# Folding the dt projection straight into token order, with the softplus on 128x16

## The chip, the cores and the metric

The program runs on one core of one Trainium2 chip. The metric is the device time of one execution in microseconds; the figure for a kernel is the median of its runs.

## The reference

One sequence of 256 tokens, 1,024 wide, goes through two transformer blocks in float32. The first block has two mixers side by side (an SSD mixer and an RWKV7 mixer) on one input projection, then an output projection and a gated feed-forward of 2,816. The second has HGRN2 and block attention, cross attention over a memory of 256 tokens, and a feed-forward of 4,096. The change touches one thin piece of the SSD mixer, the step size dt of its 8 heads:

```python
xn = _rms_norm(h, pre_mix_norm[l]); proj = xn @ w_in[l]
z, xbc, dt = jnp.split(p, [SSD_D, SSD_D + SSD_CONV_DIM], axis=-1)   # dt: 256 tokens x 8 heads
dt = jax.nn.softplus(dt + dt_bias)
A = -jnp.exp(a_log)
X = xh * dt[..., None]            # the mixer's values, scaled per token and head
a = dt * A                        # its cumulative sum over a chunk of 128 tokens gives all decays
```

## The kernel before

Everything is a hand-placed program: each engine runs a fixed list of instructions, and they wait for one another on semaphores (`mark` counts a step, `at` gives the value that it reached, `wait_ge` waits). The order of the work is the order of the calls at the end of the listing for each engine (from L3362 for ScalarE, from L3459 for VectorE), and nothing is reordered at run time. Activations lie with features on the partitions and 256 tokens along the free dimension, in tiles of 128 features. A weight is loaded in float32 in chunks of up to 2 MB into a ring of four slots, by one queue (SyncE's, L482 to L497); ScalarE makes the high float16 half (L539), VectorE the low half (L571), and TensorE multiplies each tile in three float16 products (L625). A chunk's slot is given back when its last reader is done, and only then is the next chunk's load issued.

The input projection runs tile by tile in the order k, lora, r, v, xs, bc, z (L814, `pe_project1`). The results leave PSUM by `evacuate1` on VectorE (L1036), a bank of two tiles at a time, and ScalarE (`act_kept`, L1076) and VectorE (`dve_shift`, L1083) do the token shift of the RWKV part. Between the tiles TensorE does small steps of the mixers whose inputs are ready: the dt fold (L913) after the third r tile, the low-rank products (L1637), the norms of the keys (`pe_head_norm`, L1661), the turning of v (L1790).

The dt part goes in these steps:
- After the lora tiles, 8 float32 products (L966), one for each 128 rows of the weight, go to four groups of 32 partitions of bank 5; products 0 to 3 to the left half, 4 to 7 to the right half. The 8 heads are the last 8 of each 32 columns.
- VectorE scales both halves by the norm into `dt_parts`, 128x512 (L1049).
- `pe_dt_fold` (L913) adds the four groups and the two halves by two products with a piece of the identity as weights and 256 columns moving; dt then has 8 heads on partitions and 256 tokens along.
- ScalarE adds the bias (L1134), between `act_kept(act, 2)` and the split of the xs weights (L3383). Later `act_dt`, `act_dt_log` and `dve_dt` make the softplus and the product with the rate on tiles of 8x256: four operations on ScalarE (L1140, L1141, L1143, L1148), of which one is on the 8 rates, and five on VectorE (L1166 to L1179).
- `pe_ssd` turns dt and its product with the rate into token order by four transposes (L1200, L1201), after the first z tile, and `dve_ssd` copies them out (L1268) before it scales the values (L1273). TensorE sums over tokens at L1215, after the second z tile; VectorE copies the sums out (L1279), and the decays follow from them (L1190, L1288, L1360, L1364, L1294), while the z tiles fill TensorE (L901).

`parameter_table` packs all small parameters, then x and the memory in feature order, then the final gain, in one tensor with 128 rows of 21,888 bytes. The small parameters are its first 352 columns; x begins at byte 1,408 of a row. x is loaded in three pieces at the start (L455), the memory's features by L496.

Of the kernel before, what the change touches and what calls it, by code (L numbers as in the profile page):

```python
# [17 lines left out]
ALU = mybir.AluOpType  # L18
# [5 lines left out]
P = 128  # L24
T = 256
# [37 lines left out]
    ("ssd_conv_w", 4 * 8), ("ssd_conv_b", 8), ("ssd_norm", 4), ("ssd_d", 4),  # L63
    ("ssd_dt_bias", 1), ("ssd_a_log", 1),
    ("rwkv_mu", 14), ("rwkv_w0", 4), ("rwkv_a0", 4), ("rwkv_k_k", 4), ("rwkv_k_a", 4),
# [9 lines left out]
PARAM_COLS = _n  # L75
X_AT, MEM_AT, FINAL_AT = PARAM_COLS, PARAM_COLS + KT * T, PARAM_COLS + 2 * KT * T

# [65 lines left out]
def parameter_table(inputs):  # L143

    def tiles(a):
        return np.asarray(a).reshape(-1, P).T

    def column(a):
        out = np.zeros((P, 1), np.float32)
        out[:a.shape[0], 0] = a  # L150
        return out

    a = {k: np.asarray(v) for k, v in inputs.items()}
    mu = a["rwkv_mu"][0]
    cols = {name: None for name, _ in PARAM_TILES}
    for name in cols:
        if name == "rwkv_mu":
            k0 = RW_D + 64
            al = 3 * RW_D + 64
            order = [mu[k0:k0 + RW_D], mu[RW_D:k0], mu[al:al + 64], mu[al + 64:], mu[:RW_D],  # L160
                     mu[k0 + RW_D:k0 + 2 * RW_D]]
            cols[name] = tiles(np.concatenate(order))
        elif name == "ssd_conv_w":
            cols[name] = np.concatenate([tiles(a[name][0, i]) for i in range(4)], axis=1)
        elif name == "ffn_conv_w":
            cols[name] = np.concatenate([tiles(a[name][0, i]) for i in range(3)], axis=1)
        elif name == "lb_logits_2":
            cols[name] = np.concatenate([tiles(a[name][i]) for i in range(2)], axis=1)
        elif name == "ssd_d":
            cols[name] = tiles(np.repeat(a[name][0], SSD_D // SSD_HEADS))  # L170
        elif name in ("ssd_dt_bias", "ssd_a_log"):
            cols[name] = column(a[name][0])
        else:
            cols[name] = tiles(a[name].reshape(-1))
        assert cols[name].shape[1] == dict(PARAM_TILES)[name], name
    def turned(rows):

        return rows.T.reshape(KT, P, T).transpose(1, 0, 2).reshape(P, KT * T)

    return np.ascontiguousarray(np.concatenate([*cols.values(), turned(a["x"][0]), turned(a["mem_2"][0]),  # L180
                                                np.broadcast_to(a["norm_final_2"].reshape(1, D), (P, D))], axis=1))
# [129 lines left out]
def build(nc, w, out, known):  # L311

    with ExitStack() as ctx:
# [15 lines left out]
        def halves(b):  # L329
            return banks[b][:, :].rearrange("p (i t) -> p i t", i=2)  # L330
# [21 lines left out]
        def const(name):  # L352
            a, n = CONST_AT[name]
            return consts[:, a:a + n]
# [61 lines left out]
        BTOKS = view(SOLVE + 5152, 2, SSD_STATE)  # L416
        dtT, aT, dtmp = view(SOLVE + 7168, T), view(SOLVE + 5664, T), view(SOLVE + 5920, T)
        dt_parts = view(SOLVE + 5664, 2, T)
        dtok = view(SOLVE + 6176, NC_, 8)
        atok = view(SOLVE + 6192, NC_, 8)  # L420
        cstok = view(SOLVE + 6208, NC_, 8)
        dect = view(SOLVE + 6224, 8)
        acol = view(SOLVE + 6232, 2)
        GT = A_[:, 0:2, :].rearrange("p a (b t) -> p (a b) t", t=C)
# [483 lines left out]
        def pe_dt_fold(pe):  # L908

            pe.wait_ge(*at("dt raw"))  # L910
            pe.wait_ge(*at("constants landed"))
            for i in range(2):
                mm = nc.tensor.matmul(banks[6][0:SSD_HEADS, 0:T], const("ident32")[:, BASE - SSD_HEADS:BASE],  # L913
                                      dt_parts[:, i, :], start=(i == 0), stop=(i == 1))
            mm.then_inc(*mark("proj1_dt", "dt folded"))

        def pe_project1(pe):
            pe_project1_first(pe)
            for i, (kind, j) in enumerate(TILE_OF):
# [42 lines left out]
                if kind == "lora" and j == 1:  # L962

                    for k in range(KT):
                        q = BASE * (k % 4)
                        mm = nc.tensor.matmul(halves(5)[q:q + BASE, k // 4, :], slot("w_in", "lora")[:, k, 232:264],  # L966
                                              hg[:, k, :], start=True, stop=True, tile_position=(0, q))
                    mm.then_inc(*mark("proj1_dt", "proj1 dt"))
# [70 lines left out]
        def dve_project1_rwkv(dve):  # L1039
            lora_low(dve)  # L1040
            dve.wait_ge(*at("pre_mix", "rstd"))
            for b in range(7):
# [4 lines left out]
                if b == 2:  # L1047
                    dve.wait_ge(*at("proj1 dt"))
                    nc.vector.scalar_tensor_tensor(dt_parts, halves(5), 1.0 / W_SCALE, over(rstd[:, :], 2), ALU.mult,  # L1049
                                                   ALU.mult).then_inc(*mark("dt_raw", "dt raw"))  # L1050
                if b in (0, 2):
                    split_low(dve, b // 2, range(4))
                if b == 3:
                    split_low(dve, 2, range(4))
                if b == 4:
                    dve_shift(dve, range(3))
                    bc_low(dve, (0, 1))
# [71 lines left out]

        def act_dt_bias(act):  # L1130

            act.wait_ge(*at("parameters landed"))
            act.wait_ge(*at("dt folded"))
            nc.scalar.activation(dtT[0:8, :], banks[6][0:SSD_HEADS, 0:T], ACT.Identity,  # L1134
                                 bias=par("ssd_dt_bias", 0)[0:8, :]).then_inc(*mark("dt_act", "dt biased"))

        def act_dt(act):

            act.wait_ge(*at("dt biased"))
            nc.scalar.activation(dtmp[0:8, :], dtT[0:8, :], ACT.Abs).then_inc(*mark("dt_act"))  # L1140
            nc.scalar.activation(acol[0:8, 0:1], par("ssd_a_log", 0)[0:8, :], ACT.Exp).then_inc(*mark("dt_act"))  # L1141
            act.wait_ge(*so_far("dt_act"))
            nc.scalar.activation(dtmp[0:8, :], dtmp[0:8, :], ACT.Exp, scale=-1.0).then_inc(*mark("dt_act", "dt exp"))  # L1143

        def act_dt_log(act):
            act.wait_ge(*at("dt one plus"))
            act.wait_ge(*at("mem", "squares", 1))
            nc.scalar.activation(dt_log, aT[0:8, :], ACT.Ln).then_inc(*mark("dt_act", "dt log"))  # L1148

# [11 lines left out]

        dt_log = sqs[0:8, 0, 0:T]

        def dve_dt(dve):
            dve.wait_ge(*at("dt exp"))
            nc.vector.tensor_scalar(aT[0:8, :], dtmp[0:8, :], 1.0, None, ALU.add).then_inc(  # L1166
                *mark("dt_vector", "dt one plus"))
            dve.wait_ge(*so_far("dt_vector"))

            nc.vector.scalar_tensor_tensor(dtmp[0:8, :], aT[0:8, :], -1.0, dtmp[0:8, :], ALU.add,  # L1170
                                           ALU.subtract).then_inc(*mark("dt_vector"))
            dve.wait_ge(*so_far("dt_vector"))
            nc.vector.scalar_tensor_tensor(dtT[0:8, :], dtT[0:8, :], 0.0, dtmp[0:8, :], ALU.max,
                                           ALU.subtract).then_inc(*mark("dt_vector"))
            dve.wait_ge(*so_far("dt_vector"))
            dve.wait_ge(*at("dt log"))
            nc.vector.tensor_tensor(dtT[0:8, :], dtT[0:8, :], dt_log, ALU.add).then_inc(*mark("dt_vector"))
            dve.wait_ge(*so_far("dt_vector"))
            nc.vector.tensor_scalar(aT[0:8, :], dtT[0:8, :], acol[0:8, 0:1], -1.0, ALU.mult, ALU.mult).then_inc(  # L1179
                *mark("dt_vector", "dt done"))  # L1180
# [13 lines left out]
        def pe_ssd(pe):  # L1194

            pe_z_tile(pe, 0)
            pe.wait_ge(*at("dt done"))
            pe.wait_ge(*at("v token-major", 1))
            for c in range(NC_):
                nc.tensor.transpose(banks[4][:, 8 * c:8 * c + 8], dtT[0:8, c * C:(c + 1) * C], ident[0:8, 0:8])  # L1200
                mm = nc.tensor.transpose(banks[4][:, 16 + 8 * c:24 + 8 * c], aT[0:8, c * C:(c + 1) * C],  # L1201
                                         ident[0:8, 0:8])
            mm.then_inc(*mark("ssd_pe", "ssd dt turned"))

            pe.wait_ge(*at("kk unit"))
# [6 lines left out]
            pe_z_tile(pe, 1)  # L1212
            pe.wait_ge(*at("ssd dt token-major"))
            for c in range(NC_):
# [51 lines left out]
        def dve_ssd(dve):  # L1266
            dve.wait_ge(*at("ssd dt turned"))
            nc.vector.tensor_copy(view(SOLVE + 6176, 32), banks[4][:, 0:32]).then_inc(  # L1268
                *mark("ssd_vector", "ssd dt token-major"))
            dve.wait_ge(*so_far("ssd_vector"))  # L1270
            for c in range(NC_):
# [2091 lines left out]
        def _(act):  # L3363
# [18 lines left out]
            act_kept(act, 2)  # L3382
            act_dt_bias(act)  # L3383
            split_high(act, 2, range(4))
# [171 lines left out]
```

## Time and profile before

| | us |
|---|---|
| median of 3 runs | 738.62 |
| lowest and highest run | 738.46, 740.3 |
| the profiled execution, its own time | 738.89 |
| span of the profiled execution (first to last instruction) | 737.1 |

| engine | busy us | share of the span |
|---|---|---|
| DVE (VectorE) | 563.7 | 76% |
| ACT (ScalarE) | 435.1 | 59% |
| PEld (TensorE weight loads) | 593.8 | 81% |

The granted clock of TensorE is 1.00 over the whole span. All places are given in us from the start of the span. PE is TensorE's matmuls, POOL is GpSimd, SP is SyncE, which only issues transfers. Matmuls are pipelined: the length shown for one is longer than the distance to the next, so for TensorE the distances between starts are read. L12 is line 12 of the kernel; where a helper is used by several steps, its line stands for all of them.

### The profile page before, as it was taken

What the parts mean: (1) busy time and instruction counts of PE and PEld (TensorE: products, weight loads), DVE (VectorE), ACT (ScalarE), POOL (GpSimd) and SP (SyncE); (2) the same over time, 40 slices, a digit from 0 to 9 for tenths busy, and PEclk for the clock granted to TensorE, in tenths of its full rate; (3) what the DMA queues carried; (4) which work ended last, traced back from release to release, by engine and by line L of the source; (5) the groups of instructions that cost most, each with busy time, mean ns of one, the idle gap of its engine ahead of it and who ended that gap; (6) DMA issues with size and microseconds to landing.
All of it is one profiled execution on the core that took longest, in us unless ns stands there. A gap on an engine that the chain in (4) does not pass through costs nothing.

```text
span 737.1 us, 16447 instructions
## 1 busy us (share of the span) xinstructions
PE 727.0 (99%) x7048; PEld 593.8 (81%) x7048; DVE 563.7 (76%) x895; ACT 435.1 (59%) x689; POOL 49.4 (7%) x83
## 2 busy tenths in 40 slices
PE   9999999999999999999999999999999999999997
PEld 6888878889778888888877695898888888865553
DVE  5699977777889999997568797889685676762453
ACT  5599863524748667666556572487483755653342
POOL 0000143040020000000002000003003000000000
PEclk9999999999999999999999999999999999999999
DMA  9990305321666655665780742338336264566001
GB/s 317 397 406 9 114 18 192 155 67 53 217 240 228 205 181 189 227 217 184 269 303 26 289 146 113 116 121 337 116 112 232 99 213 171 207 229 232 25 1 58
DMA packets 67145, 129.50 MB, mean 176 GB/s; under 512 B 3968, under 2 KB 28032, under 8 KB 66816
## 3 DMA queue, kind: packets, MB, share of 16 engines
q1 hardware_dynamic: 66032, 126.07, 47.4%
q0 software_dynamic: 320, 1.67, 0.7%
q8 instruction: 56, 0.92, 0.5%
q10 hardware_dynamic: 720, 0.70, 0.3%
q14 instruction: 17, 0.14, 0.1%
HBM read 127.39 MB, written 1.05 MB: 174 GB/s over the span
## 4 chain that ended last, share of the span: by engine, by line
PE 82%; DVE 9%; ACT 4%; DMA 3%; SPq 2%; issue 1%; ACTq 0%; DVEq 0%
PE bank L625 38%; PE bank L747 14%; PE bank L3200 11%; PE bank L2526 3%; PE bank L1569 3%; DMA ring<-in_w_in_dram 3%; PE bank L1550 2%; DVE arena L571 2%; PE bank L1828 1%; SPq L496 1%; PE bank L901 1%; DVE arena L1083 1%; PE bank L2006 1%; ACT arena L539 1%; DVE arena L613 1%
## 5 line engine op out<-in xcount | busy, mean ns | idle before, releaser
L625 PE MATMUL bank<-hg,arena 128*128 128x256 f16 x2496 | 275.0, 273 | 0.2 <-DVE hg L650 0.2
L625 PEld LDWEIGHTS bank<-hg,arena 128*128 128x128 f16 x2496 | 243.9, 98 | 30.5 <-issue 1.1
L571 DVE SCALAR_TENSOR_TENSOR arena<-ring,arena 128x1024 f16<-128x1024 f32 x150 | 175.6, 1226 | 60.2 <-ACT arena L539 60.2
L539 ACT ACTIVATE arena<-ring 128x1024 f16<-128x1024 f32 x150 | 146.7, 1044 | 87.9 <-PE bank L3200 37.6
L3200 PE MATMUL bank<-arena 128*128 128x512 f16 (+1 forms) x480 | 83.6, 336 | 0.0
L3200 PEld LDWEIGHTS bank<-arena 128*128 128x128 f16 x480 | 47.0, 98 | 36.1
L747 PE MATMUL bank<-arena 128*128 128x256 f16 x528 | 57.8, 273 | 0.0
L747 PEld LDWEIGHTS bank<-arena 128*128 128x128 f16 x528 | 51.7, 98 | 6.0
L558 DVE SCALAR_TENSOR_TENSOR arena<-ring,arena 128x2048 f16<-128x2048 f32 x22 | 50.4, 2292 | 0.7
L747 PE MATMUL bank<-mix,arena 128*128 128x256 f16 x384 | 42.2, 273 | 0.0
L551 ACT ACTIVATE arena<-ring 128x2048 f16<-128x2048 f32 x22 | 41.7, 1894 | 0.0
L747 PEld LDWEIGHTS bank<-mix,arena 128*128 128x128 f16 x384 | 37.6, 98 | 4.3
L625 PE MATMUL bank<-xv,arena 128*128 128x256 f16 x336 | 37.4, 273 | 0.0
L2434 DVE SCALAR_TENSOR_TENSOR arena<-arena,params 128x256 f32<-128x256 f32 x88 | 36.7, 479 | 0.7 <-ACT arena L2477 0.7
L625 PEld LDWEIGHTS bank<-xv,arena 128*128 128x128 f16 x336 | 32.6, 98 | 4.9 <-issue 0.7
L2477 ACT ACTIVATE arena<-arena,params 128x256 f32<-128x256 f32 x44 | 20.0, 500 | 27.7 <-DVE arena L2423 27.7
L3154 DVE SCALAR_TENSOR_TENSOR arena<-bank,rstd 128x512 f32<-128x512 f32 x16 | 11.0, 690 | 24.0 <-PE bank L625 16.9
L640 ACT ACTIVATE hg<-h,params 128x256 f16<-128x256 f32 x32 | 15.9, 498 | 22.2 <-DVE h L2963 11.8
L660 POOL TENSOR_TENSOR ssum<-sqs 128x256 f32<-128x256 f32 x4 | 2.9, 728 | 350.0 <-ACT sqs L644 350.0
L650 DVE SCALAR_TENSOR_TENSOR hg<-h,params,hg 128x256 f16<-128x256 f32 x32 | 20.4, 658 | 4.4 <-ACT hg L640 4.4
L1569 PE MATMUL bank<-arena,xk 128*128 128x512 f16 x96 | 21.4, 379 | 0.0
L2526 PE MATMUL bank<-arena,hg 128*128 128x512 f16 x96 | 21.2, 379 | 0.0
(419 smaller groups left out, 974.0 us busy)
## 6 DMA issues: line engine op xcount, KB each, us to landing
ring<-in_w_in_dram SPq DMA_DIRECT2D x12, 2048.0 KB, 9.3
ring<-in_ffn_w_up_dram SPq DMA_DIRECT2D x22, 1024.0 KB, 7.3
ring<-in_w_ff_dram SPq DMA_DIRECT2D x8, 2048.0 KB, 9.1
ring<-in_w_ff_dram SPq DMA_DIRECT2D x16, 1024.0 KB, 6.6
ring<-in_ffn_w_down_dram SPq DMA_DIRECT2D x11, 1024.0 KB, 5.5
ring<-in_w_out_dram SPq DMA_DIRECT2D x8, 1024.0 KB, 7.8
ring<-in_w_xk_dram SPq DMA_DIRECT2D x2, 2048.0 KB, 11.2
ring<-in_w_xv_dram SPq DMA_DIRECT2D x2, 2048.0 KB, 10.7
```

The source lines that it names most:

```text
L539: nc.scalar.activation(quarter(halves_of(chunk)[0], chunk, q), quarter(slot(*chunk), chunk, q), ACT.Copy, scale=W_SCALE).then_inc(*mark("w ...
L551: nc.scalar.activation(pair_of(halves_of(chunk)[0], chunk, q), pair_of(slot(*chunk), chunk, q), ACT.Copy, scale=W_SCALE).then_inc(*mark("w ...
L558: nc.vector.scalar_tensor_tensor(pair_of(halves_of(chunk)[1], chunk, q), pair_of(slot(*chunk), chunk, q), W_SCALE, pair_of(halves_of(chunk ...
L571: nc.vector.scalar_tensor_tensor(quarter(halves_of(chunk)[1], chunk, q), quarter(slot(*chunk), chunk, q), W_SCALE, quarter(halves_of(chunk ...
L625: mm = nc.tensor.matmul(out_, weight[a][:, k, cols], src[:, k, b, :], start=(first and i == 0), stop=(last and i == 2), skip_group_check=True)
L650: nc.vector.scalar_tensor_tensor(hg16[:, m, 1, :], h[:, m, :], par(gain, m), hg16[:, m, 0, :], ALU.mult, ALU.subtract).then_inc(*mark("nor ...
L747: mm = nc.tensor.matmul(out_, weight, moving[:, k, b, :], start=(first and n == 0), stop=(last and n == 2), skip_group_check=True)
L1569: mm = nc.tensor.matmul(banks[2 + c][:, :], mem16[:, k, x, c * C:(c + 1) * C], w_[a][:, k, :], start=(k == 0 and i == 0), stop=(k == KT - ...
L2434: nc.vector.scalar_tensor_tensor(uacc[r][:, i, :], uraw[r][:, i, tap:tap + T], par("ffn_conv_w", 2 * FFT * tap + tile0 + i), uacc[r][:, i, :],
L2477: nc.scalar.activation(uacc[r][:, i, :], uraw[r][:, i, 2:T + 2], ACT.Copy, scale=par("ffn_conv_w", 2 * 2 * FFT + 2 * p + FFT * (b % 2) + i ...
L2526: mm = nc.tensor.matmul(banks[bank][:, :], hg16[:, k, b, c * C:(c + 1) * C], w_[a][:, k, :], start=(k == 0 and n == 0), stop=(k == KT - 1 ...
L3200: mm = nc.tensor.matmul(last_bank(c, half, cols)[:, cols], hid2[:, k, x, c * C:(c + 1) * C], weight[a][:, k % 4, 512 * half + cols.start:5 ...
```

## The change

- The products 4 to 7 of dt are added in PSUM to the products 0 to 3 (same four groups of partitions, one half of the bank). `dt_parts` is 128x256 instead of 128x512.
- The fold takes `dt_parts` as weights, 128 tokens at a time, and 8 columns of the identity piece as the moving side. So dt comes out with 128 tokens on the partitions, and 2 chunks x 8 heads along: 128x16.
- The bias is added by VectorE (`dve_dt_bias`), after the evacuation of bank 4 of the projection and before its token shifts; the ScalarE step is gone.
- The softplus and the product with the rate run on 128x16; the rate's exponential on 128x8.
- The four transposes, the copy out and their waits are gone; "dt done" is waited for after the second z tile, and by VectorE before it scales the values. ScalarE's logarithm no longer waits for the memory's squares, whose buffer it used.
- The bias and the rate stand in 8 columns each, repeated on all 128 partitions. The small parameters are now 366 columns, x begins at column 384 (byte 1,536), and a row has 22,016 bytes. 14 more columns are loaded with the small parameters (L3366).

```diff
-    ("ssd_dt_bias", 1), ("ssd_a_log", 1),
+    ("ssd_dt_bias", SSD_HEADS), ("ssd_a_log", SSD_HEADS),
...
-X_AT, MEM_AT, FINAL_AT = PARAM_COLS, PARAM_COLS + KT * T, PARAM_COLS + 2 * KT * T
+X_AT = (PARAM_COLS + 63) // 64 * 64
+MEM_AT, FINAL_AT = X_AT + KT * T, X_AT + 2 * KT * T
...
-            for i in range(2):
-                mm = nc.tensor.matmul(banks[6][0:SSD_HEADS, 0:T], const("ident32")[:, BASE - SSD_HEADS:BASE],
-                                      dt_parts[:, i, :], start=(i == 0), stop=(i == 1))
+            for c in range(NC_):
+                mm = nc.tensor.matmul(banks[6][:, 8 * c:8 * c + 8], dt_parts[:, c * C:(c + 1) * C],
+                                      const("ident32")[:, BASE - SSD_HEADS:BASE], start=True, stop=True)
...
-                        mm = nc.tensor.matmul(halves(5)[q:q + BASE, k // 4, :], slot("w_in", "lora")[:, k, 232:264],
-                                              hg[:, k, :], start=True, stop=True, tile_position=(0, q))
+                        mm = nc.tensor.matmul(banks[5][q:q + BASE, 0:T], slot("w_in", "lora")[:, k, 232:264],
+                                              hg[:, k, :], start=(k < 4), stop=(k >= 4), tile_position=(0, q),
+                                              skip_group_check=True)
...
                 if b == 4:
+                    dve_dt_bias(dve)
                     dve_shift(dve, range(3))
...
-        def act_dt_bias(act):
-
-            act.wait_ge(*at("parameters landed"))
-            act.wait_ge(*at("dt folded"))
-            nc.scalar.activation(dtT[0:8, :], banks[6][0:SSD_HEADS, 0:T], ACT.Identity,
-                                 bias=par("ssd_dt_bias", 0)[0:8, :]).then_inc(*mark("dt_act", "dt biased"))
+        def dve_dt_bias(dve):
+
+            dve.wait_ge(*at("parameters landed"))
+            dve.wait_ge(*at("dt folded"))
+            nc.vector.tensor_tensor(dtok, banks[6][:, 0:NC_ * 8].rearrange("p (c h) -> p c h", c=NC_),
+                                    over(by_head("ssd_dt_bias"), NC_), ALU.add).then_inc(*mark("dt_vector", "dt biased"))
...
-            nc.scalar.activation(dtmp[0:8, :], dtmp[0:8, :], ACT.Exp, scale=-1.0).then_inc(*mark("dt_act", "dt exp"))
+            nc.scalar.activation(dt_small, dt_small, ACT.Exp, scale=-1.0).then_inc(*mark("dt_act", "dt exp"))
...
             act.wait_ge(*at("dt one plus"))
-            act.wait_ge(*at("mem", "squares", 1))
-            nc.scalar.activation(dt_log, aT[0:8, :], ACT.Ln).then_inc(*mark("dt_act", "dt log"))
+            nc.scalar.activation(dt_log, dt_one, ACT.Ln).then_inc(*mark("dt_act", "dt log"))
...
-            nc.vector.tensor_scalar(aT[0:8, :], dtT[0:8, :], acol[0:8, 0:1], -1.0, ALU.mult, ALU.mult).then_inc(
+            nc.vector.scalar_tensor_tensor(atok, dtok, -1.0, over(acol, NC_), ALU.mult, ALU.mult).then_inc(
                 *mark("dt_vector", "dt done"))
...
             pe_z_tile(pe, 0)
-            pe.wait_ge(*at("dt done"))
             pe.wait_ge(*at("v token-major", 1))
-            for c in range(NC_):
-                nc.tensor.transpose(banks[4][:, 8 * c:8 * c + 8], dtT[0:8, c * C:(c + 1) * C], ident[0:8, 0:8])
-                mm = nc.tensor.transpose(banks[4][:, 16 + 8 * c:24 + 8 * c], aT[0:8, c * C:(c + 1) * C],
-                                         ident[0:8, 0:8])
-            mm.then_inc(*mark("ssd_pe", "ssd dt turned"))
...
-            pe.wait_ge(*at("ssd dt token-major"))
+            pe.wait_ge(*at("dt done"))
...
         def dve_ssd(dve):
-            dve.wait_ge(*at("ssd dt turned"))
-            nc.vector.tensor_copy(view(SOLVE + 6176, 32), banks[4][:, 0:32]).then_inc(
-                *mark("ssd_vector", "ssd dt token-major"))
-            dve.wait_ge(*so_far("ssd_vector"))
+            dve.wait_ge(*at("dt done"))
...
-            act_dt_bias(act)
```

## Rows read from the trace of the kernel before

**Rows 1.** The page, part 1: busy us, share of the span, instructions of each engine.
```profile
PE 727.0 (99%) x7048; PEld 593.8 (81%) x7048; DVE 563.7 (76%) x895; ACT 435.1 (59%) x689; POOL 49.4 (7%) x83
```

**Rows 2.** Windows: stretch, length, busy us by engine, granted clock, DMA share, GB/s.
```profile
20.00:30.00 10.00, 10.00 (x100) 8.31 (x99) 6.71 (x8) 4.70 (x6) 1.76 (x3) 1.00 1.05 391
...
640.00:670.00 30.00, 30.00 (x204) 19.90 (x202) 15.28 (x16) 14.17 (x18) 0.00 (x0) 1.00 0.60 224
```

**Rows 3.** Chain of waits in order of time, 13 to 67: start us, us, what.
```profile
13.39 18.63 DMA ring<-in_w_in_dram
32.04 2.61 ACT arena L539 x3
...
37.53 0.35 ACT arena L1134
...
65.99 0.42 ACT arena L696
```

**Rows 4.** Timeline of PE, 33 to 67: start, us, instruction, [idle before <-releaser].
```profile
33.56 1.03 PE L913 MATMUL bank<-arena,consts 128*8 128x256 f32 x4
34.53 18.51 PE L625 MATMUL bank<-xv,arena 128*128 128x256 f16 x168
...
66.46 0.71 PE L1661 MATMUL bank<-arena,consts 32*128 32x256 f32 x8 [0.23 <-ACT arena L696]
```

**Rows 5.** Timeline of ACT, 37 to 46.
```profile
37.44 0.45 ACT L1134 ACTIVATE arena<-bank,params 8x256 f32<-8x256 f32 x1
...
42.38 1.99 ACT L1012 ACTIVATE mix<-ring 128x1024 f16<-128x1024 f32 x2
```

**Rows 6.** Timeline of DVE, 38 to 47.
```profile
38.86 4.63 DVE L571 SCALAR_TENSOR_TENSOR arena<-ring,arena 128x1024 f16<-128x1024 f32 x4 [0.51 <-ACT arena L539]
...
44.01 2.46 DVE L1083 SCALAR_TENSOR_TENSOR arena<-arena,params 128x256 f32<-128x256 f32 x6
```

**Rows 7.** Line L496, loads issued from 24 to 27: first and last start, issue to landing.
```profile
L496 SPq DMA_DIRECT2D ring<-in_w_in_dram x1: 800/800/800, 25.7 to 25.7; - x1
...
DMA to landing us min/median/max: 16.2/16.9/17.5
```

**Rows 8.** Timeline of ACT, 67 to 71.
```profile
67.27 0.19 ACT L1709 ACTIVATE small<-small 128x4 f32<-128x4 f32 x1
67.36 0.40 ACT L1140 ACTIVATE arena<-arena 8x256 f32<-8x256 f32 x1
...
69.98 0.42 ACT L1148 ACTIVATE sqs<-arena 8x256 f32<-8x256 f32 x1 [0.42 <-DVE arena L1166]
```

**Rows 9.** Timeline of DVE, 69 to 79.
```profile
69.68 0.27 DVE L1166 TENSOR_SCALAR arena<-arena 8x256 f32<-8x256 f32 x1
...
71.60 2.45 DVE L1118 SCALAR_TENSOR_TENSOR arena<-arena,params 128x256 f32<-128x256 f32 x6
...
76.18 2.56 DVE L1118 SCALAR_TENSOR_TENSOR arena<-arena,params 128x256 f32<-128x256 f32 x6 [0.41 <-ACT arena L1108]
78.66 0.19 DVE L1268 COPY arena<-bank 128x32 f32<-128x32 f32 x1
```

**Rows 10.** Timeline of DVE, 82.
```profile
82.48 0.17 DVE L1279 COPY arena<-bank 128x16 f32<-128x16 f32 x1
```

**Rows 11.** Timeline of ACT, 83 to 88.
```profile
84.00 1.14 ACT L1360 ACTIVATE arena<-bank,arena 128x128 f32<-128x128 f32 x4 [2.26 <-DVE arena L1288]
```

**Rows 12.** Timeline of PE, 76 to 89.
```profile
76.78 0.22 PE L1200 MATMUL bank<-consts,arena 8*128 8x8 f32 x1
...
77.12 1.09 PE L1210 MATMUL bank<-consts,arena 128*128 128x128 f32 x8
...
81.51 0.51 PE L1215 MATMUL bank<-arena,consts 128*128 128x8 f32 x4
81.87 1.14 PE L1223 MATMUL bank<-arena 128*128 128x128 f32 x8
...
88.29 0.65 PE L1190 MATMUL bank<-consts,arena 128*128 128x128 f32 x4 [0.29 <-DVE arena L1298]
```

More of the change, by code:

```diff
@@ L171, in parameter_table @@
         elif name in ("ssd_dt_bias", "ssd_a_log"):
-            cols[name] = column(a[name][0])
+            cols[name] = np.broadcast_to(a[name][0].reshape(1, SSD_HEADS), (P, SSD_HEADS))
         else:
@@ L178, in turned @@
         return rows.T.reshape(KT, P, T).transpose(1, 0, 2).reshape(P, KT * T)
-    return np.ascontiguousarray(np.concatenate([*cols.values(), turned(a["x"][0]), turned(a["mem_2"][0]),
+    spare = np.zeros((P, X_AT - PARAM_COLS), np.float32)
+    return np.ascontiguousarray(np.concatenate([*cols.values(), spare, turned(a["x"][0]), turned(a["mem_2"][0]),
                                                 np.broadcast_to(a["norm_final_2"].reshape(1, D), (P, D))], axis=1))
@@ L416, in build @@
         BTOKS = view(SOLVE + 5152, 2, SSD_STATE)
[L417 to L420, printed above, removed]
+        dt_parts = view(SOLVE + 7168, T)
+        dtok, atok, dt_small, dt_one, dt_log = [view(SOLVE + 7168 + 16 * i, NC_, 8) for i in range(5)]
+        acol = view(SOLVE + 7248, 8)
         cstok = view(SOLVE + 6208, NC_, 8)
         dect = view(SOLVE + 6224, 8)
-        acol = view(SOLVE + 6232, 2)
         GT = A_[:, 0:2, :].rearrange("p a (b t) -> p (a b) t", t=C)
@@ L1048, in dve_project1_rwkv @@
                     dve.wait_ge(*at("proj1 dt"))
-                    nc.vector.scalar_tensor_tensor(dt_parts, halves(5), 1.0 / W_SCALE, over(rstd[:, :], 2), ALU.mult,
+                    nc.vector.scalar_tensor_tensor(dt_parts, banks[5][:, 0:T], 1.0 / W_SCALE, rstd[:, :], ALU.mult,
                                                    ALU.mult).then_inc(*mark("dt_raw", "dt raw"))
@@ L1128, in dve_z, with by_head @@
                 *mark("proj1_scaled", "proj1 out", b))
-        def act_dt_bias(act):
-            act.wait_ge(*at("parameters landed"))
-            act.wait_ge(*at("dt folded"))
-            nc.scalar.activation(dtT[0:8, :], banks[6][0:SSD_HEADS, 0:T], ACT.Identity,
-                                 bias=par("ssd_dt_bias", 0)[0:8, :]).then_inc(*mark("dt_act", "dt biased"))
+        def by_head(name):
+            return params[:, PARAM_AT[name]:PARAM_AT[name] + SSD_HEADS]
+        def dve_dt_bias(dve):
[3 more added lines that the diff above has]
+                                    over(by_head("ssd_dt_bias"), NC_), ALU.add).then_inc(*mark("dt_vector", "dt biased"))
         def act_dt(act):
             act.wait_ge(*at("dt biased"))
-            nc.scalar.activation(dtmp[0:8, :], dtT[0:8, :], ACT.Abs).then_inc(*mark("dt_act"))
-            nc.scalar.activation(acol[0:8, 0:1], par("ssd_a_log", 0)[0:8, :], ACT.Exp).then_inc(*mark("dt_act"))
+            nc.scalar.activation(dt_small, dtok, ACT.Abs).then_inc(*mark("dt_act"))
+            nc.scalar.activation(acol, by_head("ssd_a_log"), ACT.Exp).then_inc(*mark("dt_act"))
             act.wait_ge(*so_far("dt_act"))
-            nc.scalar.activation(dtmp[0:8, :], dtmp[0:8, :], ACT.Exp, scale=-1.0).then_inc(*mark("dt_act", "dt exp"))
+            nc.scalar.activation(dt_small, dt_small, ACT.Exp, scale=-1.0).then_inc(*mark("dt_act", "dt exp"))
         def act_dt_log(act):
             act.wait_ge(*at("dt one plus"))
-            act.wait_ge(*at("mem", "squares", 1))
-            nc.scalar.activation(dt_log, aT[0:8, :], ACT.Ln).then_inc(*mark("dt_act", "dt log"))
+            nc.scalar.activation(dt_log, dt_one, ACT.Ln).then_inc(*mark("dt_act", "dt log"))
         def act_ssd_silu(act, n):
@@ L1160, in act_z_silu @@
                     *mark("z_silu", "z silu", n))
-        dt_log = sqs[0:8, 0, 0:T]
         def dve_dt(dve):
             dve.wait_ge(*at("dt exp"))
-            nc.vector.tensor_scalar(aT[0:8, :], dtmp[0:8, :], 1.0, None, ALU.add).then_inc(
-                *mark("dt_vector", "dt one plus"))
+            nc.vector.tensor_scalar(dt_one, dt_small, 1.0, None, ALU.add).then_inc(*mark("dt_vector", "dt one plus"))
             dve.wait_ge(*so_far("dt_vector"))
-            nc.vector.scalar_tensor_tensor(dtmp[0:8, :], aT[0:8, :], -1.0, dtmp[0:8, :], ALU.add,
-                                           ALU.subtract).then_inc(*mark("dt_vector"))
+            nc.vector.scalar_tensor_tensor(dt_small, dt_one, -1.0, dt_small, ALU.add, ALU.subtract).then_inc(
+                *mark("dt_vector"))
             dve.wait_ge(*so_far("dt_vector"))
-            nc.vector.scalar_tensor_tensor(dtT[0:8, :], dtT[0:8, :], 0.0, dtmp[0:8, :], ALU.max,
-                                           ALU.subtract).then_inc(*mark("dt_vector"))
+            nc.vector.scalar_tensor_tensor(dtok, dtok, 0.0, dt_small, ALU.max, ALU.subtract).then_inc(
+                *mark("dt_vector"))
             dve.wait_ge(*so_far("dt_vector"))
             dve.wait_ge(*at("dt log"))
-            nc.vector.tensor_tensor(dtT[0:8, :], dtT[0:8, :], dt_log, ALU.add).then_inc(*mark("dt_vector"))
+            nc.vector.tensor_tensor(dtok, dtok, dt_log, ALU.add).then_inc(*mark("dt_vector"))
             dve.wait_ge(*so_far("dt_vector"))
-            nc.vector.tensor_scalar(aT[0:8, :], dtT[0:8, :], acol[0:8, 0:1], -1.0, ALU.mult, ALU.mult).then_inc(
+            nc.vector.scalar_tensor_tensor(atok, dtok, -1.0, over(acol, NC_), ALU.mult, ALU.mult).then_inc(
                 *mark("dt_vector", "dt done"))
```

## The prediction

> **What bounds the kernel now.** I read the page first, then windows for the loads, then the chain of waits, then the timelines of PE, ACT and DVE around the dt steps. The page puts PE at 99% busy [rows 1]; that invites the reading that every TensorE instruction taken out is time gained. It isn't so in the stretch of this change, because the length of a matmul in the profile hides short gaps. Four things are to be seen.
>
> (1) Up to 32 us the loads set the pace. The window from 20 to 30 has a DMA share of 1.05 [rows 2], and the chain rests on one load of w_in from 13.39 until 32.0, the v weights [rows 3].
>
> (2) From 32 to 66.4 the chain is in ScalarE and VectorE, which split the weights and shift the tokens. ScalarE's dt bias is itself a link of it, 0.35 us at 37.53 [rows 3], and the chain comes back to TensorE only at 66.4, where L1661 waited 0.23 us for ScalarE's L696 [rows 3, 4]. TensorE is dense before that: 168 products from 34.53 [rows 4].
>
> (3) From 66.4 to 77 TensorE sets the end. The four dt transposes stand in that stretch, from 76.78 to 77.12 [rows 12].
>
> (4) From 77 to 88.3 the chain goes by VectorE and ScalarE again: ScalarE sat idle 2.26 us until VectorE's L1288 released L1360 at 84.00 [rows 11], and TensorE waited 0.29 us at 88.29 for VectorE's L1298 [rows 12]. What a dt edit is worth is how much earlier L1190 at 88.29 starts; behind it nothing is changed, the loads are released by steps that move with it, so that shift is carried to the end of the 737.1 us.
>
> **The change part by part.**
>
> *The products of dt (L966) and their evacuation.* Eight products as before, to the same four groups of partitions; only the target of the last four changes. I cost it at nothing, within 0.1 us either way. The evacuation shrinks from 128x512 to 128x256. VectorE then has nothing until 33.12, when it waits for the v weights that land at 32.0 [rows 3], so that covers it. Without this cover it would be worth about 0.3 us, half of a step like L1126.
>
> *The fold.* Before: four records of 256 columns, 33.56 to 34.53, 0.97 us [rows 4]. After: two float32 products with 128x128 weights and 8 columns moving. L1215 is that same shape and takes from 81.51 to 81.87, 0.36 us [rows 12]. TensorE is 0.61 us earlier behind it. What it meets next is L1661, which already waits 0.23 us; the wait grows by what TensorE gains over ScalarE. So 0.61 us is worth nothing as long as ScalarE is last at 66.4; if TensorE were last, all of it would count.
>
> *The bias.* ScalarE loses one instruction, 37.44 to the next start at 37.79: 0.35 us [rows 3, 5]. The first xs split is ready 0.35 us sooner, and VectorE, which waited 0.51 us for it [rows 6], starts at 38.51 instead of 38.86. ScalarE's next step for a load is L1012 at 42.38 [rows 5], now at 42.03. Its bc weights were issued at 25.73 and took 16.2 us, to 41.9; the other 17.5 in that answer can't be theirs, as it would end behind their first use [rows 7]. So they are there, with 0.1 us to spare. VectorE gains an instruction ahead of L1083 at 44.01 [rows 6]: 128x16 out of PSUM, as L1279, 0.17 us, of which about 0.1 keeps the engine from the next [rows 10]. Its waits are long over: the fold is done by about 34.2, and the step stands at 43.7. Behind it are queued the six shifts, and for them ScalarE's L1614; ScalarE reaches L1614 only behind its own two L1012 and a table load, so VectorE's 0.1 lies beside those. TensorE's low-rank product at 53 now waits for this step of VectorE, nine us after it. Value taken: 0.35 us at 66.4. Bounds: 0.18 (0.35 less 0.17, if VectorE is last), and 0 if the bc weights land half a us later in another run.
>
> *The softplus.* ScalarE's three steps on 8x256 take 0.40 to 0.42 us; a short one, L1709, takes 0.19 [rows 8]. That is about 0.2 us each, 0.6 us. VectorE's five steps run from 69.68 to 71.60, 1.92 us [rows 9]; five steps of 0.17 us [rows 10] that wait for one another make about 1.0. So VectorE is 0.9 us freer. Next, though, VectorE's taps at 76.18 already waited 0.41 us for ScalarE's L1108 [rows 9], and ScalarE comes to L1108 behind the turning of v, which TensorE's order sets. Both engines' savings go into waits there. Value taken: nothing; bounds 0 and 0.9 us.
>
> *The transposes and the copy.* TensorE: 76.78 to 77.12, 0.34 us [rows 12]. VectorE: L1268 goes, 78.66 to the next start at 78.88, 0.22 us [rows 9]. The two streams meet at the sums (L1190), L1283 and L1288. TensorE comes there 0.35 + 0.34 = 0.69 us earlier, VectorE 0.35 + 0.22 = 0.57. The later one decides: 0.57. "dt done" is reached near 70.2, the first wait for it is VectorE's at about 78 and TensorE's at about 80.8, so neither waits.
>
> *The parameters.* 14 more columns on 128 rows are 7 KB, 0.02 us at 391 GB/s [rows 2]. x's 1 MB lies in the saturated stretch (2.7 us at that rate), the memory's too. Does its new place change its speed? A row of w_in has 3,336 floats, 13,344 bytes, no multiple of 256; rows of the last feed-forward's second weight have 4,096. The first moved 391 GB/s at a share of 1.05, the second 224 at 0.60 [rows 2]: 372 and 373 per unit of busy engine. So I take nothing for the place, with bounds of 0.3 us either way. The Trainium skill states otherwise (DMA: Bandwidth & Descriptors, How a descriptor splits into AXI transactions): a descriptor that doesn't start at a multiple of 256 bytes has its first transaction start at the multiple below, and pays for the bytes before it. Every other row of x was half such a unit off, 1,408 bytes plus 21,888 for each row, and now none is; by that page x would be some 3% cheaper, an estimate of 0.08 us, and the sum 0.65 instead of 0.57. The two equal rates of this trace don't bear the page out.
>
> **Sum.** 0.35 + 0.22 = 0.57 us. The profiled execution took 738.89 (span 737.1 and 1.8 around it), so 738.3 by its own measure; the median of the runs lies 0.27 below it, at 738.62, and gives 738.05. I say 738.0.
>
> **The rivals.**
>
> *More is on the path than the chain shows.* If TensorE is last throughout, as 99% busy suggests, the fold and the transposes count in full: 0.61 + 0.34 = 0.95, 737.7. If it is VectorE, 0.35 + 0.9 + 0.22 = 1.5, 737.1. For it: the waits against it are small (0.23, 0.41, 0.29 us) and one execution's. Against: all of them point the same way.
>
> *Nothing arrives.* The bc weights land later than 41.9, the wait takes the place of the bias, and the 0.22 is lost in the zigzag from 82 to 88: 738.6.
>
> *The transfers gain.* If x's place matters more than I take, its 2.7 us and as much for the memory shrink. A tenth of x is 0.3 us (737.7 with the forecast). To be over 0.3% faster, 1.7 us of x's 2.7 would have to go.
>
> *Slower.* The place is the loads before 32 us. All rows of x begin at another spot of the memory and 22,016 bytes apart; if its 1 MB, ahead of the v weights in the same engines, moves more slowly, the chain from 13.39 to 32.0 is longer by just that, since the share is at its limit. It decides from 0.57 us, x a fifth slower. A third slower is 0.9 us: 738.6 + 0.9 - 0.6 = 738.9. Against it: the equal rates above.
>
> **How the numbers follow.** Forecast 0.5 (737.8 to 738.3), more on the path 0.2 (737.1 to 737.7), nothing arrives 0.14, the transfers gain 0.08, slower 0.08. The runs of before themselves spread from 738.46 to 740.3. So 736.7 to 739.4 should hold the time 8 times in 10. A measurement of this kernel tells about 0.3%, 2.2 us, from no change. No sum above reaches that: faster by more needs most of x's transfer to go (0.05) or several savings together that I count as covered (0.04); slower by more needs x at half its rate or a disturbance of the loads that I don't see (0.05). That leaves 0.86 within.
>
> **What would show each step.** The fold in about 0.36 us, and TensorE's wait at L1661 about 0.5 us instead of 0.23, from ScalarE's L696. L696 0.35 us earlier, L1012 at about 42.0; if it says that it waited for a load, the bias was hidden. No dt transposes; VectorE idle over 1 us before the taps at 76, still for ScalarE's L1108; if that idle is gone, the softplus did count. L1360 at about 83.4 and L1190 at about 87.7, and the same distance from there to the end. x's pieces landing as before (2.8, 3.9 and 6.5 us) if their place does nothing. I am wrong if the v weights land at another time than 32.0 by more than 0.3 us, or if the distance behind L1190 changes by as much as the shift itself.

## The result and the profile after

The kernel after takes 740.09 us, median of 18 runs (739.32 to 742.36), against 738.46 for the kernel before (18 runs): the ratio is 1.0027, 95% interval 1.0021 to 1.0033. It is slower by 1.6 to 2.4 us where I forecast 0.6 us faster, and outside my range. The profiled execution took 741.68 us, its span is 739.9. The 18 executions form two groups: eleven from 739.3 to 740.1 with a mean granted clock of 0.998 or more (the lower group), seven from 741.5 to 742.4 with 0.997 or less (the upper group). The profiled one is of the upper group. So there are two things to explain: about 1.3 us that the lower group loses too (its median is 739.8), and about 2 us more in the upper group.

The loads of the kernel after, in the windows that answer to [rows 2], and the whole saturated stretch (columns as there):

```profile
20.00:30.00 10.00, 10.00 (x100) 8.31 (x98) 6.77 (x9) 4.70 (x6) 1.76 (x3) 1.00 1.06 369
...
16.00:40.00 24.00, 23.56 (x221) 20.08 (x219) 14.97 (x16) 14.87 (x21) 1.76 (x3) 1.00 1.04 379
```

The same window of the kernel before, from its own trace:

```profile
16.00:40.00 24.00, 24.00 (x219) 19.92 (x217) 15.76 (x16) 15.67 (x23) 1.76 (x3) 1.00 1.05 400
```

The engines of the loads are as busy as before and move 5% less. That is the first thing to see: 379 GB/s at a share of 1.04, against 400 at 1.05. It isn't x's load alone: the packets of 2,048 bytes from 16 to 56 us, the stretch of w_in's loads, last 84.9 ns on the mean before and 89.1 after, in the packet records of the two traces. So what ScalarE waits for comes later (its timeline after, with the first split of the xs weights and of the bc weights, and line L496 for the bc load):

```profile
38.30 3.90 ACT L539 ACTIVATE arena<-ring 128x1024 f16<-128x1024 f32 x4 [0.57 <-DMA ring<-in_w_in_dram]
...
43.71 2.00 ACT L1013 ACTIVATE mix<-ring 128x1024 f16<-128x1024 f32 x2 [0.72 <-DMA ring<-in_w_in_dram]
```
```profile
L496 SPq DMA_DIRECT2D ring<-in_w_in_dram x1: 572/572/572, 25.4 to 25.4; - x1
DMA to landing us min/median/max: 18.2/18.2/18.2
```

The xs split starts at 38.30 where it started at 37.79; the bc load takes 18.2 us instead of 16.2 [rows 7], and its first use, 42.38 in [rows 5], is at 43.71, now behind a wait of 0.72 us for the load. Then TensorE, the rows that answer to [rows 4] and [rows 12]:

```profile
33.23 0.58 PE L913 MATMUL bank<-consts,arena 128*128 128x8 f32 x4
33.67 18.50 PE L625 MATMUL bank<-xv,arena 128*128 128x256 f16 x168
...
67.80 0.71 PE L1652 MATMUL bank<-arena,consts 32*128 32x256 f32 x8 [2.44 <-ACT arena L696]
68.45 7.08 PE L625 MATMUL bank<-xv,ring 128*128 128x256 f16 x48
...
91.07 0.65 PE L1191 MATMUL bank<-consts,arena 128*128 128x128 f32 x4 [0.39 <-DVE arena L1289]
```

Two losses stand here. TensorE waits 2.44 us for ScalarE's key rates (before: 0.23): its 168 products started 0.86 us earlier (33.67 against 34.53), and the rates come 1.34 us later (67.80 against 66.46). And the 48 products after this wait take 7.08 us; in every other trace of this study but two they take 5.41 or 5.42. The windows say why (the granted clock is the third number from the end):

```profile
69.00:72.50 3.50, 3.50 (x19) 2.49 (x17) 3.36 (x13) 2.56 (x5) 0.00 (x0) 0.52 0.00 0
72.50:76.00 3.50, 3.50 (x33) 3.21 (x32) 2.35 (x6) 1.58 (x6) 0.00 (x0) 0.99 0.00 0
```

For 3.4 us, from 69.1 to 72.5, the clock is at its lower level, 1.2 instead of 2.4 GHz. That costs 1.7 us. From L1190 or L1191 to the end these two profiles take the same time: 737.1 - 88.29 = 648.8 before, 739.9 - 91.07 = 648.8 after. So the 2.8 us between the two spans lie ahead of 91 us: 1.3 from ScalarE's later key rates (L1652 at 67.80 against 66.46), 1.7 from the clock, less 0.2 for the dt steps.

The dt steps themselves did what the diff says (ScalarE, then VectorE):

```profile
68.70 0.20 ACT L1145 ACTIVATE arena<-arena 128x16 f32<-128x16 f32 x1
...
71.23 0.22 ACT L1152 ACTIVATE arena<-arena 128x16 f32<-128x16 f32 x1 [0.31 <-DVE arena L1168]
```
```profile
71.03 0.16 DVE L1168 TENSOR_SCALAR arena<-arena 128x16 f32<-128x16 f32 x1
...
71.95 2.46 DVE L1120 SCALAR_TENSOR_TENSOR arena<-arena,params 128x256 f32<-128x256 f32 x6
...
79.19 2.56 DVE L1120 SCALAR_TENSOR_TENSOR arena<-arena,params 128x256 f32<-128x256 f32 x6 [1.80 <-ACT arena L1110]
```

### The profile page after: what moved, and what is told of

Same layout as the page of the kernel before. It is cut to its first block, busy times and chain, and to the rows that moved or that the text cites. A ratio compares the mean times of both kernels' runs of the same rounds, so it can differ in the third digit from the quotient of the medians.

```text
span 739.9 us, 16436 instructions
## 1 busy us (share of the span) xinstructions
PE 726.8 (98%) x7044; PEld 593.9 (80%) x7044; DVE 562.3 (76%) x895; ACT 434.1 (59%) x688; POOL 49.4 (7%) x83
## 3 DMA queue, kind: packets, MB, share of 16 engines
HBM read 127.39 MB, written 1.05 MB: 174 GB/s over the span
## 4 chain that ended last, share of the span: by engine, by line
PE 85%; DVE 8%; ACT 4%; DMA 2%; issue 1%; DVEq 0%
PE bank L625 39%; PE bank L747 13%; PE bank L3191 11%; PE bank L2517 3%; PE bank L1560 3%; DMA ring<-in_w_in_dram 2%; PE bank L1541 2%; PE bank L882 1%; DVE arena L571 1%; PE bank L1819 1%; PE bank L1997 1%; DVE arena L613 1%; PE bank L2731 1%; PE bank L3014 1%; PE bank L1971 1%
## 5 line engine op out<-in xcount | busy, mean ns | idle before, releaser
L551 ACT ACTIVATE arena<-ring 128x2048 f16<-128x2048 f32 x22 | 41.7, 1894 | 0.0
```

The source lines that it names most:

```text
L551: nc.scalar.activation(pair_of(halves_of(chunk)[0], chunk, q), pair_of(slot(*chunk), chunk, q), ACT.Copy, scale=W_SCALE).then_inc(*mark("w ...
```

## The experiments

Each ratio below is to the kernel before on the same chip, with its 95% interval. Two theories stood at first. Layout: the new place of the parameters in memory slows the loads. Clock: TensorE, ahead by its shorter fold, idles longer and loses its clock. Each diff shows the part of the edit that matters. Where the width of the parameter tile is set by hand, the load of the small parameters is written to fill only its first PARAM_COLS columns, so it moves the same bytes as without the edit.

**The layout alone.** The kernel before with

```diff
-X_AT, MEM_AT, FINAL_AT = PARAM_COLS, PARAM_COLS + KT * T, PARAM_COLS + 2 * KT * T
+X_AT = 384
+MEM_AT, FINAL_AT = X_AT + KT * T, X_AT + 2 * KT * T
```

> The kernel before with only the layout of the parameter tensor changed: 32 spare columns, x at byte 1,536, rows of 22,016 bytes; all instructions as before. Layout theory (the new place of the parameters slows the loads, and the splits of the weights with them): slower by 1 to 2 us, xs and bc landing over 1 us later than 36.9 and 41.9. Clock theory (the kernel after is slower because TensorE, 0.6 us ahead, sits idle longer at the key norm and its clock is then lowered) and my prediction: no change, within 0.3 us.

The parameter tensor gets 32 spare columns to fit, so x begins at byte 1,536 of a row of 22,016 bytes, as in the kernel after. Measured: 738.52 us, ratio 1.0001 (0.9993 to 1.0010). Its loads move 400 GB/s from 16 to 40 us, as before. The layout in memory does nothing that shows.

**The dt change alone, with the old layout.** The kernel after with

```diff
-    ("ssd_dt_bias", SSD_HEADS), ("ssd_a_log", SSD_HEADS),
+    ("ssd_dt_bias", 1), ("ssd_a_log", 1),
...
-X_AT = (PARAM_COLS + 63) // 64 * 64
+X_AT = PARAM_COLS
...
+        dt_rows = sb("dt_rows", 2 * SSD_HEADS)
```

> The kernel after, but with the parameter tensor laid out as before (21,888 bytes a row); the repeated bias and rate come from a small tensor of their own, 8 KB, by one more transfer. Layout theory: no slower than before, by my sum 0.6 us faster. Clock theory: slower than before by 1 us or more, granted clock under 0.999 in most executions.

The repeated bias and rate come from a small tensor of their own, by one more transfer into `dt_rows`. Measured: 741.34 us, ratio 1.0030 (1.0021 to 1.0038); 6 of 11 executions have a clock of 0.997 or less. Its loads are slow:

```profile
16.00:40.00 24.00, 23.37 (x219) 20.02 (x218) 14.71 (x16) 14.62 (x21) 1.77 (x3) 1.00 1.04 378
```

That was against both theories: 378 GB/s with the old layout, and no clock theory explains slow loads at 16 us, before any dt step. What this kernel shares with the kernel after, besides the dt steps, is more columns in SBUF ahead of the ring of weights: 16 here, 14 there.

**Filling the wait.** The kernel after with 16 unused float16 products behind the 20th tile, ahead of `pe_head_norm`:

```diff
+                    pe_fill(pe, 16)
                     pe_head_norm(pe)
```

> The kernel after, and 16 extra products of 128x256 float16 (1.7 us, results not used) on TensorE right ahead of the wait for the key rates. Clock theory: the clock stays at its upper level, so it is faster than the kernel after by 1 to 2 us, although TensorE has more to do; the fill costs at most what of it outlasts the wait. Layout theory: no better than the kernel after, or slower by up to 1 us.

Measured: 740.13 us, ratio 1.0020 (1.0011 to 1.0029). Its median is near that of the lower group of the kernel after (739.8); one of 11 executions has a clock of 0.997 or less. The wait is 0.28 us and the 48 products behind it are at full speed:

```profile
67.87 0.71 PE L1659 MATMUL bank<-arena,consts 32*128 32x256 f32 x8 [0.28 <-ACT arena L696]
68.52 5.41 PE L625 MATMUL bank<-xv,ring 128*128 128x256 f16 x48
```

So the clock makes the upper group, and not the loss that all executions share (1.8 us in this run). The lower group of the kernel after itself was never profiled, so its wait at this place isn't known.

**Restoring the fold's length.** The kernel after with 6 such products behind the fold (`pe_fill(pe, 6)` behind `pe_dt_fold(pe)`):

> The kernel after, and 6 extra products of 128x256 float16 (0.65 us, results not used) right behind the fold, so that TensorE is as late there as before. Clock theory: the wait at the key norm is as short as before, the clock stays up, 1 us or more faster than the kernel after. Layout theory: as the kernel after.

Measured: 740.28 us, ratio 1.0027 (1.0018 to 1.0035). Three of 11 executions are in the upper group; its profiled one had the clock up throughout and a wait of 0.77 us. The median is as slow as the kernel after, so the lead of TensorE isn't the loss.

**The place in SBUF.** The tiles lie one behind another in the order of L335 on, and the tile of the parameters is PARAM_COLS wide. By the program's own allocation the ring began at byte 28,416 of a partition, 111 times 256; with 366 columns (as with 352 and 16) it begins at 28,480, 64 bytes further, and x and every tile behind it moved as much. The traces hold no addresses, so these two figures are the allocation's alone; the four shifts compared below, by 0, 64, 128 and 256 bytes, follow from the widths in the edits. The theory: loads to targets that don't begin at a multiple of 256 are slower. The kernel after with

```diff
-        params = sb("params", PARAM_COLS)
+        params = sb("params", 416)
```

> The kernel after, with one difference: the SBUF tile of the parameters is 416 columns wide instead of 366 (the added ones are never used), so that the ring, x and every later target of a load begin at a multiple of 256 bytes in SBUF, as in the kernel before; in the kernel after they begin 64 bytes behind one. Place theory (the 14 added columns moved every load's target, and the loads got slower): w_in's 2,048-byte packets take 84 ns again, bc lands near 41.9, and by the sum of my prediction it is 0.6 us faster than the kernel before. Clock theory (TensorE's longer wait at the key norm costs it all): still 1 us or more slower than before.

and the kernel before with 368, and with 384, in the same place:

> The kernel before with the SBUF tile of the parameters 368 columns wide instead of 352, nothing else: every later target begins 64 bytes behind a multiple of 256. Place theory: slower by 1.5 to 3 us, bc landing at 43 or later, TensorE's wait for L696 over 1 us, the granted clock in some executions under 1. Clock theory, or any theory by which the dt steps themselves do it: as before.

> The kernel before with the SBUF tile of the parameters 384 columns wide: targets 128 bytes behind a multiple of 256. Place theory, if any distance from a multiple of 256 does it: as slow as with 64 bytes. If only half multiples of 128 do it: no change.

Measured: 738.59 us, ratio 1.0002 (0.9993 to 1.0011) for the kernel after with its ring back at a multiple; 740.02, ratio 1.0021 (1.0012 to 1.0030), for the kernel before moved by 64 bytes; 740.10, ratio 1.0025 (1.0016 to 1.0034), moved by 128. In this order, each from its own trace:

```profile
16.00:40.00 24.00, 23.92 (x224) 20.52 (x223) 16.03 (x17) 15.96 (x22) 1.77 (x3) 1.00 1.05 400
```
```profile
16.00:40.00 24.00, 24.00 (x218) 19.78 (x217) 15.69 (x16) 15.70 (x23) 1.77 (x3) 1.00 1.04 377
```
```profile
16.00:40.00 24.00, 23.90 (x215) 19.57 (x214) 15.36 (x16) 15.45 (x22) 1.76 (x3) 1.00 1.04 378
```

The theory holds in both directions: an unused column width gives the kernel before the shared loss, 1.6 us, with no instruction added or taken out (with 368 columns no execution had a clock under 0.998; with 384, two of 11 had 0.997 or less), and takes it from the kernel after. The wait is where the kernel after has it, here in the kernel before with 368 columns:

```profile
43.24 2.01 ACT L1012 ACTIVATE mix<-ring 128x1024 f16<-128x1024 f32 x2 [0.69 <-DMA ring<-in_w_in_dram]
```

Over all 14 profiles of this study the first bc split starts from 41.7 to 42.4 us in the seven whose ring is at a shift of 0 or 256 bytes, and from 43.2 to 44.0 in the seven at 64 or 128. Every tile behind the parameters moved together, so the runs don't separate the ring from x or the arena. The engines' own steps don't show the shift: the four xs splits take 3.88 or 3.90 us and the 48 products 5.41 or 5.42 at either place.

But the forecast of 0.6 us faster than before isn't met. The bc split of the kernel after with 416 columns waits for its load, as in the layout run of the kernel before (the first line is that of the kernel before with its layout changed, the second of the kernel after with 416 columns):

```profile
41.97 2.00 ACT L1014 ACTIVATE mix<-ring 128x1024 f16<-128x1024 f32 x2 [0.33 <-DMA ring<-in_w_in_dram]
```
```profile
42.26 2.01 ACT L1013 ACTIVATE mix<-ring 128x1024 f16<-128x1024 f32 x2 [0.32 <-DMA ring<-in_w_in_dram]
```

**The fold, with the loads in order.** 416 columns and `pe_fill(pe, 6)` behind the fold:

> The kernel after with the 416-column tile, and 6 extra float16 products (0.65 us) right behind the fold. Tests the step of my prediction that the shorter fold is worth nothing: the same time as with the 416 columns alone, within 0.2 us. If TensorE is last in this stretch, 0.6 us slower; if TensorE's longer idling costs clock, faster.

Measured: 738.65 us, ratio 1.0003 (0.9994 to 1.0012), against 738.59 without the fill. TensorE's wait at the key norm is gone in its profile, and the time is the same: the shorter fold is worth nothing that shows.

**All targets at multiples of 256, and the best version.** By the same allocation the constants and the small parameters were loaded 128 bytes behind a multiple in the kernel before too. With

```diff
+        sb("spacer", 32)
         consts = sb("consts", CONST_COLS)
-        params = sb("params", PARAM_COLS)
+        params = sb("params", 384)
```

all of them begin at one, and the ring 256 bytes behind its first place. The kernel after so, the same with `pe_fill(pe, 8)` ahead of the key norm, the kernel before so, and the kernel after once more on that chip:

> The kernel after with 32 unused columns ahead of the constants in SBUF and a parameter tile of 384: now the constants and the small parameters too, not only the ring, x and what follows, are loaded to multiples of 256 bytes (in the kernel before these two lay 128 bytes behind one). Place theory: the 1.3 MB of constants take some 5% less of the saturated stretch, about 0.2 us, so bc lands near 41.8 and the time is 0.2 us below the kernel after with the 416-column tile (738.6): 738.3 to 738.4, level with before. If only the ring's targets matter: as with 416 columns.

> The same, and 8 extra float16 products (0.9 us) on TensorE right ahead of the wait for the key rates, to shorten its idling there to about 0.3 us. If long idling there is what halves the clock for some us behind it in part of the executions: no execution with a granted clock of 0.997 or less, the highest times 1 us lower, the median 0.2 to 0.4 us lower, and so the fastest of all, 738.0. If the clock falls for other reasons: as without the fill.

> The kernel before with the same 32 columns ahead of the constants and a parameter tile of 384, so that all these loads go to multiples of 256 bytes. Against the first kernel of this call it shows what the dt change is worth when the loads are equal: by what bc's landing leaves of my sum (the bias hidden by the load, the copy counted), the kernel after is 0.1 to 0.3 us faster; by the full sum 0.6 us.

> The kernel after unchanged, once more, on the same chip as the three others. Slower than before by 1.5 to 2.5 us, in two groups of executions: near 739.8 at a granted clock of 0.998 or more, near 741.8 at 0.997 or less.

Measured, to 738.45 for the kernel before: 738.12 (ratio 0.9998, 0.9989 to 1.0007), 738.63 (1.0001, 0.9992 to 1.0010), 738.59 (1.0003, 0.9994 to 1.0012) and, with 5 runs, 741.55 (1.0037, 1.0024 to 1.0049). The first has the lowest median of the kernels made here and beats the kernel after clearly, but can't be told from the kernel before, nor from the kernel before so padded. The constants' target is worth nothing that shows: 399 GB/s from 16 to 40 us. With 8 filling products no execution of 11 has a clock of 0.997 or less, against two of 11 without, which is too few to tell; the median isn't lower.

## Why the prediction was wrong, point by point

**The parameters: the step that failed.** I priced the 14 columns as 7 KB more to load and asked whether x's new place in memory matters, with 0.3 us either way. The layout run shows no change (its interval is 0.5 us down to 0.7 us up), so that part stands. What I left out is the other end: PARAM_COLS is also the width of the SBUF tile that lies ahead of the ring, so every load of the program got a new target. I put that at nothing without a reason. 5 to 6% less rate in the saturated stretch makes the bc weights land at 43.6 instead of 41.9, and the chain behind 42 us starts with them: +1.6 us in the median (the kernel before moved by 64 bytes). Both kernel texts were there to be compared, so the shift could have been seen before the run.

The rule of the Trainium skill that I set aside (DMA: Bandwidth & Descriptors, How a descriptor splits into AXI transactions) speaks of what a transaction reads, and says nothing of the target of a load. The source side shows nothing here: 372 and 373 GB/s per busy share in [rows 2], 400 GB/s with either layout. The target side shows 400 against 377 and 378. If that rule of the Trainium skill is carried over to the target, which is my step and not its own, a run of 2,048 bytes that starts 64 bytes behind a multiple pays for 64 bytes more, an estimate of 3%, and at 128 bytes of 6%. Measured are 5 to 6% less rate at both, and packets longer by 4.9% at 64 bytes (89.1 ns) and 5.5% at 128 (89.6 ns). So the rule carried over gives the direction, and its size fits one of the two; what makes the loads slower inside the chip stays open.

**The slower rival** named the right resource (the loads ahead of 42 us, full to the brim, each delay counted one to one) and the wrong mechanism (x's reads), with 0.08.

**The bias, 0.35 us.** It is 0 with the loads in order. I had seen that L1012 would then stand 0.1 us behind its load's landing and took that as enough. But the profile of the kernel before was the odd one. It is the only one of the 14 whose bc split doesn't wait for its load; the others wait 0.31 to 0.36 us with the ring at a shift of 0 or 256 bytes and 0.68 to 0.72 at 64 or 128, with the old dt steps as with the new. Its v split started at 32.04, in the six other profiles with fast loads at 28.8 to 31.2, so ScalarE was late in it and met a load that had already landed. In the layout run and in the kernel before with all targets in order ScalarE is early without the edit. This was my second bound, and it is the one that holds. One profile was read as if it were the kernel.

**The transposes and the copy, 0.22 us more.** Right, as far as L1190. From the first bc split to L1190 or its like it is 45.93 us in the layout run (41.97 to 87.90) and 45.77 with 416 columns (42.26 to 88.03). It is 45.9 to 46.0 in all five profiles with the old dt steps and 45.7 to 45.8 in the six with the new ones and the clock up: 0.2 us, all that the dt change gives.

**The fold.** 0.36 or 0.37 us in six of the nine profiles that have the new one, as forecast, and 0.44 in three, the kernel after among them (33.23 to 33.67); worth nothing, as said. But I took idling of TensorE as free. With the late loads the wait became 2.44 us, and behind waits of 2.44, 2.46 and 2.06 us (kernel after, dt change alone, kernel after once more) the clock fell at 68.4 to 69.1 us in all three profiles; behind waits of 0 to 1.22 us it fell there in none of the other eleven. 11 of the 23 executions of the kernel after have a clock of 0.997 or less, 1 of 11 with the wait filled. How long a wait it takes can't be said from this, and the fall isn't bound to this place or to the change. One profile with all targets in order, its wait here only 0.94 us, has its fall at 107.3, within a wait of 0.96 us (106.6 to 107.6) that the kernels before and after have there too, without a fall. And of the kernel before, run beside the experiments on three chips, 8 of 94 executions have a clock of 0.996 and take 739.6 to 740.7 us. So the change with its late loads makes a fall more frequent; it doesn't introduce it. That three of 11 executions fall although the fold's length is restored stays unexplained.

**The softplus.** VectorE's five steps take 0.92 us (71.03 to 71.95; forecast 1.0), ScalarE's 0.20 and 0.22. VectorE's wait ahead of the taps grew from 0.41 to 1.80 us and ends with ScalarE's L1110; with 416 columns and the clock up it is 1.42. Off the path, as said.

**The distance from L1190 to the end** is 648.8 us in the two profiles compared first, and I had said that it wouldn't change. That match is luck. In the profile of the kernel before, one split (L1521, at 151.85) started 0.28 us later behind L1190 than in the layout run; the four other profiles with the old dt steps have 648.5 or 648.6. With the new ones it is 648.8 or 648.9 in seven of nine (648.5 in the run of the dt change alone, 650.3 where the clock fell at 107.3). The difference lies in the last 7 us, in two waits of ScalarE in the last norm. They add to 1.12 us with the old steps and to 1.40 or 1.41 with the new, in all but the run of the dt change alone (1.12). The second of the two in the layout run, then with 416 columns:

```profile
731.64 0.42 ACT L3292 ACTIVATE sqs<-xk 128x256 f32<-128x256 f32 x1 [0.50 <-DVE small L3274]
```
```profile
732.04 0.42 ACT L3281 ACTIVATE sqs<-xk 128x256 f32<-128x256 f32 x1 [1.06 <-DVE small L3266]
```

The first of the two is 0.61 and 0.34 us. So of the forecast 0.57 us the bias was hidden behind the load, and the 0.2 us that did arrive at L1190 are lost again, by 0.28 us, at the very end. That fits the medians: the kernel after with its loads in order is level with the kernel before and not 0.2 us faster. Why ScalarE starts that step later isn't known. The dt steps with the old layout and their own small tensor don't have it, and the shift of the tiles alone doesn't do it (the kernel before with 368 or 384 columns has 1.12).

## What to carry to other kernels

A column added to one SBUF tile moves every tile behind it. In a stretch where the loads are at their limit, compare the start of each load's target with a multiple of 256 bytes before and after the edit, and compare GB/s at equal DMA share in one window of both traces. That pair of numbers, 400 and 379, says at once that the transfers themselves are slower and not started later; here it took a kernel with nothing but a wider tile to name the cause. An engine's saving ahead of a wait isn't free of effect: in the three profiles with the longest waits of TensorE the clock fell behind them. And a margin of 0.1 us at a wait, read from one profile, is no margin: the two other profiles of the kernel before with fast loads, with its layout changed and with all targets in order, both show the wait.

## What the runs showed of the hardware

- With the targets in SBUF at 64 or 128 bytes behind a multiple of 256 the loads from 16 to 40 us move 377 to 379 GB/s at a share of 1.04 (seven profiles), at a multiple 399 to 402 at 1.04 or 1.05 (seven). x at byte 1,408 in rows of 21,888 bytes or at 1,536 in rows of 22,016 makes no difference beside that: 400 both. The mean of the 2,048-byte packets from 16 to 56 us is 84.9 to 85.2 ns against 88.9 to 89.6.
- After a wait of over 2 us TensorE ran 3.4 us at 1.2 GHz, which began 0.5 to 1.3 us after work had resumed (three profiles), and 48 products took 6.90 to 7.08 us instead of 5.41. A fourth profile has 3.4 us at 1.2 GHz from 107.3 us, begun within a wait of 0.96 us.
